# Query norms of a gated delta scan: sums by a still block of ones, a root over a whole bank, and the first decay rows fetched earlier

## The reference, cut to what matters

```python
def _l2norm(x):
    xf = x.astype(jnp.float32)
    return (xf * lax.rsqrt(jnp.sum(xf * xf, axis=-1, keepdims=True) + EPS)).astype(x.dtype)
...
    q = chunks(q) * (DK ** -0.5)
    k = chunks(k)
    gc = jnp.cumsum(chunks(g[..., None])[..., 0], axis=-1)
    diff = gc[..., :, None] - gc[..., None, :]
    decay = jnp.where(tri, jnp.exp(jnp.where(tri, diff, 0.0)), 0.0)
```

## Time and profile before

| what | value |
|---|---|
| median of three runs | 2818.96 us (2818.36 to 2821.8) |
| profiled execution, its own time | 2814.47 us |
| span of that execution | 2812.6 us |
| mean granted clock of TensorE, share of full speed | 0.961 |
| PE busy | 2601.9 us, 93% |
| DVE busy | 1643.9 us, 58% |
| POOL busy | 1150.0 us, 41% |
| ACT busy | 633.1 us, 23% |
| scan stages, where they start | at about 1339.5 us and 1634.7 us of the span |

### The profile page before, as it was taken

The page is one execution under the profiler, slowest core; times in us unless marked ns, Lnnn a source line. Parts: engine busy times, 40 slices in busy tenths (PEclk is TensorE's granted clock), DMA queues, the critical chain, the costliest instruction groups (busy, mean ns, idle before and its releaser), DMA issues. The chain is left out here.

```text
span 2812.6 us, 45432 instructions
## 1 busy us (share of the span) xinstructions
PE 2601.9 (93%) x18626; PEld 2175.0 (77%) x18626; DVE 1643.9 (58%) x2507; ACT 633.1 (23%) x1229; POOL 1150.0 (41%) x930
## 2 busy tenths in 40 slices
PE   8989999989889999989799979978798999899998
PEld 6778888778568888867788869864686888688887
DVE  7958658472658838667454656533576516563451
ACT  4121111110322101134343344301354100110000
POOL 3544554554044554524331433111333545444453
PEclk9999999999999999989799989989999999999999
DMA  4224343322033334221011101101110222222222
GB/s 155 96 99 154 115 142 136 104 76 75 1 112 135 126 128 148 85 75 46 25 40 47 60 24 41 47 17 38 49 26 31 77 103 90 90 84 96 94 101 75
DMA packets 51317, 229.68 MB, mean 82 GB/s; under 512 B 5297, under 2 KB 12481, under 8 KB 32577
## 3 DMA queue, kind: packets, MB, share of 16 engines
q1 hardware_dynamic: 51136, 227.10, 23.4%
HBM read 224.91 MB, written 2.17 MB: 81 GB/s over the span
## 5 line engine op out<-in xcount | busy, mean ns | idle before, releaser
L246 POOL TENSOR_TENSOR ring_rounded<-ring,ring_rounded 128x512 fp32r<-128x512 f32 (+2 forms) x715 | 935.5, 1340 | 1141.5 <-DVE ring_rounded L237 1133.0
L286 PE MATMUL psum<-arena_rounded,ring_rounded 128*128 128x512 f32 (+1 forms) x2820 | 1100.6, 390 | 61.0 <-PEq L515 13.7
L287 PE MATMUL psum<-arena_rounded,ring_rounded 128*128 128x512 f32 (+1 forms) x2820 | 1091.3, 387 | 0.0
L288 PE MATMUL psum<-arena_rounded,ring_rounded 128*128 128x512 f32 (+1 forms) x2820 | 1090.2, 387 | 0.0
L286 PEld LDWEIGHTS psum<-arena_rounded,ring_rounded 128*128 128x128 f32 x2820 | 536.5, 190 | 182.3 <-issue 45.6
L288 PEld LDWEIGHTS psum<-arena_rounded,ring_rounded 128*128 128x128 f32 x2820 | 536.2, 190 | 107.6
L287 PEld LDWEIGHTS psum<-arena_rounded,ring_rounded 128*128 128x128 f32 x2820 | 536.7, 190 | 104.8 <-issue 1.5
L237 DVE CAST ring_rounded<-ring 128x2048 fp32r<-128x2048 f32 (+4 forms) x191 | 212.3, 1111 | 676.8 <-PE psum L288 618.0
L713 ACT ACTIVATE arena<-psum,vectors 128x512 f32<-128x512 f32 x88 | 68.6, 782 | 409.8 <-PE psum L288 409.8
L329 DVE TENSOR_TENSOR arena_rounded<-arena,arena_rounded 128x512 fp32r<-128x512 f32 (+2 forms) x113 | 125.3, 1109 | 3.9
L327 DVE CAST arena_rounded<-arena 128x512 fp32r<-128x512 f32 (+2 forms) x113 | 114.1, 1010 | 9.3 <-DVE arena L743 1.0
(11 more groups left out here) (403 smaller groups left out, 3058.6 us busy)
## 6 DMA issues: line engine op xcount, KB each, us to landing
ring<-in_w_up SPq DMA_DIRECT2D x44, 1024.0 KB, 4.8
arena<-in_w_mod SPq DMA_DIRECT2D x48, 512.0 KB, 3.4
ring<-in_w_down SPq DMA_DIRECT2D x32, 704.0 KB, 4.0
ring<-in_w_mup SPq DMA_DIRECT2D x16, 1024.0 KB, 4.9
ring<-in_w_mdown SPq DMA_DIRECT2D x16, 1024.0 KB, 4.8
ring<-in_w_gdn SPq DMA_DIRECT2D x12, 1024.0 KB, 4.8
ring<-in_w_lru_in SPq DMA_DIRECT2D x10, 1024.0 KB, 4.8
ring<-in_w_odd_in SPq DMA_DIRECT2D x10, 1024.0 KB, 4.7
```

The source lines that it names most:

```text
L246: last = pool.tensor_tensor(self.rounded(low), raw, self.rounded(high).bitcast(F32), ALU.subtract)
L286: pe.matmul(out, r(wh), r(xh), start=start, stop=False)
L287: pe.matmul(out, r(wh), r(xl), start=False, stop=False)
L288: return pe.matmul(out, r(wl), r(xh), start=False, stop=stop)
```

## The change

The queries' norm takes another layout. For each head, one product has the ones, broadcast to 128x32, as the stationary operand, and the squares of all 512 tokens move. The four heads write to four different quarters of the 128 output partitions. `qmean` is then 128x512: in quarter h, each of 32 rows holds the 512 sums of head h. DVE fills a 128x512 tile with -0.5 and adds EPS into another; POOL's `pow` runs on 128x512; the Newton step, its last operation now holding the scale, runs on 128x512 in two halves, at levels 3 and 4. The spread is one product for a head, with the 32 rows of its quarter as contraction and 512 moving columns. The tiles of the norm moved from `small` into the arena, and other tiles were placed anew.

The fetch of the two first decay rows, and the bar on them, moved into the in-projection stage, after the values' transposes, into the area where the values had been. For that the values' transposes all stand in the first half of unit 5. ACT's six copies of value tokens stand in one piece.

The diff, cut to its core:

```diff
+SCAN_TILES = [[4, 5, 0, 1, 2, 3], [5, 4, 3, 2, 1, 0]]
 class TokenTiles:
+        self.decays = [m.at(VT_AT + GH * P * d, GH, P) for d in range(2)]
 def gdn_in_stage
+        def beside_first(t, k):
+            if k in (1, 3, 5):
+                turn_keys(3 * t + k // 2)
+        def beside_last(t, k):
+            if t == 0 and k >= 2:
+                turn_values(k - 2)
 (pool)
+        for d in range(2):
+            pool.wait_ge(m.sem("rowsin"), m.count("rowsin", 16 * (d + 1)))
+            e = tok.decays[d]
+            pool.tensor_tensor(e, e, m.bar[:, d, :]..., ALU.add).then_inc(m.up("barred"), 1)
 (sp)
+        sp.wait_ge(m.sem("turned"), m.count("turned", 2 * NA))
+        for d in range(2):
+            sp.dma_start(tok.decays[d]..., decay_rows(gc_rows, group, SCAN_TILES[d][0], d)
+                         ).then_inc(m.up("rowsin", 16), 16)
+            sp.wait_ge(m.sem("rowsin"), m.count("rowsin", 16 * (d + 1)))
 def gdn_scan_stage
+    qmean, qroot, qtmp = qsq[0:3]
+    klen, qhalf = m.small[:, K_LEN:K_LEN + GH * NA], qsq[3]
+        b["EA"] = [tok.decays[d], m.at(at[5], GH, P)]
+    quarter = [slice(32 * h, 32 * h + 32) for h in range(GH)]
 (pe: query_sums)
-                for i in range(NT):
-                    j = NT * h + i
-                    last = pe.matmul(m.psum[:, MB, j:j + 1], qsq[h][:, i * P:(i + 1) * P], m.ones[:, 0:1],
-                                     start=True, stop=True)
+                last = pe.matmul(m.psum[quarter[h], MB, :], m.ones[:, 0:1].broadcast_to([P, 32]), qsq[h],
+                                 start=True, stop=True)
 (pe: query_spread)
-            for i in range(NT):
-                last = pe.matmul(bank(d, MB)[:, i, :], qroot[:, j:j + 1].broadcast_to([P, P]), m.ident[:, :], ...)
+            r = quarter[h]
+            pe.matmul(m.psum[:, 4 * d + MB, :], m.ident[r, 32 * h:32 * h + 1].broadcast_to([32, P]), qroot[r, :], ...)
 (pool)
-        barred(0, 0)
-        barred(0, 1)
             if t == 0:
+                pool.wait_ge(m.sem("qhalf"), m.count("qhalf", 1))
                 pool.wait_ge(m.sem("qmean"), m.count("qmean", 1))
                 pool.tensor_tensor(qroot, qmean, qhalf, ALU.pow).then_inc(m.up("qroot"), 1)
 (dve)
+        def query_roots(k):
+            if k == 3:
+                dve.wait_ge(m.sem("qroot"), m.count("qroot", 1))
+                dve.tensor_tensor(qtmp, qroot, qroot, ALU.mult)
+                dve.tensor_tensor(qtmp, qtmp, qmean, ALU.mult)
+                return
+            dve.tensor_scalar(qtmp, qtmp, -0.5 * DK ** -0.5, 1.5 * DK ** -0.5, ALU.mult, ALU.add)
+            dve.tensor_tensor(qroot, qroot, qtmp, ALU.mult).then_inc(m.up("qrstd"), 1)
+                    dve.memset(qhalf, -0.5).then_inc(m.up("qhalf"), 1)
+                    dve.tensor_scalar(qmean, m.psum[:, MB, :], EPS, None, ALU.add).then_inc(m.up("qmean"), 1)
-                if (t, k) == (0, 4):
-                    query_roots()
+                if (t, k) in ((0, 3), (0, 4)):
+                    query_roots(k)
```

More of the change, by code:

```diff
@@ L1517 @@
 K_SS, K_ROOT, K_TMP, K_LEN, K_HALF = 64, 88, 112, 136, 160
-Q_MEAN, Q_ROOT, Q_TMP = 24, 40, 64
 WORK_AT = 6144
@@ L1523, with decay_rows @@
 GC_ROWS_AT = 17408 + 6 * 96
+SCAN_TILES = [[4, 5, 0, 1, 2, 3], [5, 4, 3, 2, 1, 0]]
+def decay_rows(gc_rows, group, n, d):
+    c = n * 16 + d * 8 + GH * group
+    return bass.AP(tensor=gc_rows.tensor, offset=c * P, ap=[[0, P], [1, GH * P]])
 class TokenTiles:
@@ L1763, in queries @@
                     last = tile(unit, t, k, 0)
-                    if k in (1, 3, 5):
-                        beside(3 * t + k // 2)
+                    beside(t, k)
                 last.then_inc(m.up("done"), 1)
@@ L1809, in pe @@
             else:
-                queries(unit, turn_keys if unit.u == 4 else turn_values)
+                queries(unit, beside_first if unit.u == 4 else beside_last)
             if not bd:
@@ L1889, in act @@
         tap(us[4], 1)
-        token(6)
-        token(7)
-        token(8)
+        for n in range(NA):
+            token(NA + n)
         tap(us[5], 0)
         silu(us[4], 0)
-        token(9)
         silu(us[4], 1)
-        token(10)
-        token(11)
         tap(us[5], 1)
@@ L2031, in pool @@
             m.pool_unit(pool, unit)
+        for d in range(2):
+            pool.wait_ge(m.sem("rowsin"), m.count("rowsin", 16 * (d + 1)))
+            e = tok.decays[d]
+            pool.tensor_tensor(e, e, m.bar[:, d, :].rearrange("p (a b) -> p a b", a=1).broadcast_to([P, GH, P]),
+                               ALU.add).then_inc(m.up("barred"), 1)
     def sp(sp):
@@ L2041, in sp @@
             sp.wait_ge(m.sem("gcstored"), m.count("gcstored", 16))
+        sp.wait_ge(m.sem("turned"), m.count("turned", 2 * NA))
+        for d in range(2):
+            sp.dma_start(tok.decays[d].rearrange("p a b -> p (a b)"), decay_rows(gc_rows, group, SCAN_TILES[d][0], d)
+                         ).then_inc(m.up("rowsin", 16), 16)
+            sp.wait_ge(m.sem("rowsin"), m.count("rowsin", 16 * (d + 1)))
     run_stage(m, dict(sp=sp, pe=pe, act=act, dve=dve, pool=pool))
@@ L2057, in gdn_scan_stage @@
     tok = TokenTiles(m, group)
[L2058 to L2061, removed]
+    places = [512 * i for i in range(24)] + [VT_AT + 512 * i for i in range(2, 6)]
+    qsq = [m.at(places[24 + h], T) for h in range(GH)]
+    qmean, qroot, qtmp = qsq[0:3]
+    klen, qhalf = m.small[:, K_LEN:K_LEN + GH * NA], qsq[3]
     B = []
     for d in range(2):
-        at = places[13 * d:13 * d + 13]
+        at = places[12 * d:12 * d + 12]
         b = {name: m.at(at[i], GH, P) for i, name in enumerate(("ZF", "QE", "R", "KD"))}
-        b["EA"] = [m.at(at[4], GH, P), m.at(at[5], GH, P)]
-        b["QK"] = [m.at(at[6], GH, P), m.at(at[7], GH, P), m.at(at[10], GH, P)]
+        b["EA"] = [tok.decays[d], m.at(at[5], GH, P)]
+        b["QK"] = [m.at(at[6], GH, P), m.at(at[7], GH, P), m.at(at[4], GH, P)]
         b["Z1"], b["ZC"] = m.at(at[8], GH, HB), m.at(at[8] + GH * HB, GH, HB)
         b["XC"], b["YC"] = m.at(at[9], GH, HB), m.at(at[9] + GH * HB, GH, HB)
-        b["S"] = [m.at(at[11], GH, P), m.at(at[12], GH, P)]
+        b["S"] = [m.at(at[10], GH, P), m.at(at[11], GH, P)]
         B.append(b)
-    tiles = [[4, 5, 0, 1, 2, 3], [5, 4, 3, 2, 1, 0]]
+    tiles = SCAN_TILES
+    quarter = [slice(32 * h, 32 * h + 32) for h in range(GH)]
     LEVELS = 5
@@ L2094, in sp @@
     def sp(sp):
-        def rows(n, d):
-            c = n * 16 + d * 8 + GH * group
-            return bass.AP(tensor=gc_rows.tensor, offset=c * P, ap=[[0, P], [1, GH * P]])
         def decays(t, d):
-            sp.dma_start(B[d]["EA"][t % 2].rearrange("p a b -> p (a b)"), rows(tiles[d][t], d)).then_inc(
+            sp.dma_start(B[d]["EA"][t % 2].rearrange("p a b -> p (a b)"), decay_rows(gc_rows, group, tiles[d][t], d)).then_inc(
                 m.up(f"rowsin{t % 2}{d}", 16), 16)
         def queries(t, d):
-            sp.dma_start(B[d]["QE"].rearrange("p a b -> p (a b)"), rows(tiles[d][t], d)).then_inc(
+            sp.dma_start(B[d]["QE"].rearrange("p a b -> p (a b)"), decay_rows(gc_rows, group, tiles[d][t], d)).then_inc(
                 up("qrowsin", d, 16), 16)
-        for t in range(2):
-            for d in range(2):
-                decays(t, d)
+        for d in range(2):
+            decays(1, d)
         for t in range(1, NA + 1):
@@ L2274, in query_spread @@
                 pe.wait_ge(m.sem("qscaled"), m.count("qscaled", h - 1))
-            for i in range(NT):
[L2276 to L2279, removed]
+            r = quarter[h]
+            pe.matmul(m.psum[:, 4 * d + MB, :], m.ident[r, 32 * h:32 * h + 1].broadcast_to([32, P]), qroot[r, :],
+                      start=True, stop=True).then_inc(m.up("qspread"), 1)
         gram(0, 0)
@@ L2335, in decay @@
             e = B[d]["EA"][t % 2]
-            act.wait_ge(sem("barred", d), count("barred", d, t + 1))
+            if t:
+                act.wait_ge(sem("barred", d), count("barred", d, t))
             for h in range(GH):
@@ L2374, in barred @@
             e = B[d]["EA"][t % 2]
-            pool.wait_ge(m.sem(f"rowsin{t % 2}{d}"), m.count(f"rowsin{t % 2}{d}", 16 * (t // 2 + 1)))
+            pool.wait_ge(m.sem(f"rowsin{t % 2}{d}"), m.count(f"rowsin{t % 2}{d}", 16 * ((t - 1) // 2 + 1)))
             pool.tensor_tensor(e, e, wide(m.bar[:, d, :]), ALU.add).then_inc(up("barred", d), 1)
@@ L2492, in output @@
                 dve.tensor_tensor(out, out, bank(d, MB), ALU.add).then_inc(up("oadd", d), 1)
[L2494 to L2498, removed]
+        def query_roots(k):
+            c = m.vchain
+            if k == 3:
+                dve.wait_ge(m.sem("qroot"), m.count("qroot", 1))
+                dve.tensor_tensor(qtmp, qroot, qroot, ALU.mult).then_inc(c.up(), 1)
+                dve.wait_ge(c.sem, c.now())
+                dve.tensor_tensor(qtmp, qtmp, qmean, ALU.mult).then_inc(c.up(), 1)
+                return
+            dve.wait_ge(c.sem, c.now())
```

(11 more changed lines are left out.)

## The result

The changed kernel takes 2951.57 us (median of four runs, 2950.48 to 2954.84), the kernel before 2818.66 us (four runs, 2813.67 to 2821.8). The ratio is 1.0475, with a 95% interval of 1.0457 to 1.0493: it is slower. The forecast was 2961 us with a range of 2948 to 3012. By the medians the loss is 132.9 us, where the forecast had 142. The profiled execution has a span of 2953.0 us, 140.4 more than before; the sum had 141.3. The two profiled executions lie apart by more than the medians because the one before is 4.2 us under its median and the one after is the longest of its four, 3.3 us above.

The account below looks back on a forecast made before the run. POOL's root on 512 columns was to stall each scan: 67.3 + 72.0 + 4 (clock) - 2 (spread) = 141.3 us on 2814.5, plus 4.5 to the median, given as 2961 us; range 2948 to 3012.

Parts of the forecast that it names:

- The root's length: POOL's `pow` on 128x512: 383 + 158 n ns plus one step of 0.84 us, together 82.1 us.
- a step: POOL's root: 0.84 us above the line for 24 and 32 columns, added once for 512 columns.
- recurring step: POOL's root: the step comes again or columns cost 196 to 209 ns; 100.4 to 107.3 us, 2997 to 3011; 29 in 100.
- When it starts, and the stall: DVE waits for the root before step 1's triangles: root starts at 1354.2, triangles 67.3 and 72.0 us later in the two scans.
- The rest: Outside the stall: PE's lower clock after it costs 4 us, the spread gains 2 us; the in-projection costs nothing.
- The total: Whole kernel: 141.3 us more on an execution of 2814.5, plus 4.5 to the median; 2961 us given.
- Sums: PE's four head sums at each scan's start run side by side in 2.0 us; one after another 7.8.
- the rival where the root is short: POOL's root stays under some 6 us and hidden; gains of 8.2 and 5.1 us leave 2806 us; 4 in 100.
- the first rival: POOL's root takes 100.4 to 107.3 us, by a recurring step or dearer columns; 2997 to 3011 us; 29 in 100.

## Why the prediction was right, and where it wasn't

- **The root's length.** 82.17 us measured, 82.1 forecast. The slope of 158 ns was right and is what carried it. The 0.84 us added for a step was wrong in kind: width brings no step of that size, and at 512 columns an excess of 0.89 us, 15 small steps of 59 ns, stands in its place. The two agree by chance. The chance of 29 in 100 for a recurring step rested on the same misreading of the earlier trace rows. Those rows are also not all: the kernel before has a root of 10 columns as well, 1961 ns where the line gives 1963, and seven of 4 columns, mostly 1.01 to 1.04 us (the line gives 1.02).
- **When it starts, and the stall.** The root was to start 14.7 us after the scan and started 14.5 after. The triangle of step 1 was to be 67.3 and 72.0 us late and was 66.9 and 71.4 late (1438.14 and 1800.23, less the 0.68 and 67.83 us by which the scans began later). The releaser is the root, in both.
- **The rest.** +2 us forecast, for the clock less the spread. After the triangle the trace shows +0.2 and +1.2.
- **The total.** The sum had 141.3 us, and the two profiles differ by 140.4. The medians differ by 132.9, so the closeness is in part luck with the executions that were profiled. The 4.5 us added from one execution to the median did not come back, as the profiled execution after lay above its median. The forecast of 2961 is 9.4 us over the measured median.
- **Sums.** 2.0 us forecast, 1.83 and 1.55 measured.
- **The gains, in the rival where the root is short.** This sum failed: 13.3 us, and the kernel without the root gained 20.6 by its profile. To the triangle of step 1 it was 9.2 and 6.6 us earlier (7.2 and 4.1 in the sum), behind it 3.9 and 1.0 (1.0 each). The terms that were too small: the rounds between the sums and the masks of level 3 were put at no gain and took 1.6 and 1.2 us less, with the clock higher; in the second scan the sums took 1.06 us and not 2.0; and the spread was put at 1 us a scan, where in the first scan at the full clock two pairs of 1.13 replace 2.46 and 2.05, 2.3 us. Of the 3.9 behind the triangle, 2.0 are there by the triangle of step 2; the rest is later and isn't explained. The forecast didn't suffer, since what is faster between the root's start and its end gains nothing.

On the page that I had set beside the earlier trace rows, the measurement decides: 82.17 us, and not the 5.1 of the estimate, so the branching figure of the Trainium skill ("GPSIMD Engine Reference", section 3.1) does not cover `pow`. The prediction says that this estimate would give the sum of the first rival; it is the second, the short root.

## What to carry to other kernels

Before a tile is widened to use all columns or partitions, look at which engine's operation costs by the column: a layout that saves PE 5 us may hand POOL 496 more columns at 158 ns each. Fit a line to every size of the same operation in the trace, and treat a point above the line as a question rather than as a law. A term hidden before must be compared with its cover (here 6.1 and 5.0 us from the root's start to the first that needs it, in the kernel without the root), and past that it counts in full.

## What was not expected of the hardware

- Sixteen single-column float32 products, 7.0 us of busy PE, left the clock at 0.50 in the first scan of both kernels that have them; four products of 512 columns on four quarters, 1.83 us, had it at 1.00 by their end in the same place. The clock's gain reached beyond the sums.
- DVE's operations on 128x512 from and to SBUF took 0.69 and 0.42 us alone, and up to 1.41 and 1.15 beside POOL's multiplications of 128x512. Those of 128x16 took 0.17 alone and up to 0.96 beside them.
- A logarithm and an exponential on ACT loaded a table each, 1.28 us twice.
